# Stick-breaking layer: the output units of token half 0 woven into the last head pair's attention steps, their squares on GpSimd

## The reference

```python
h = rmsnorm(x, norm_g[2])
q, k, v, g = jnp.split(h @ w_in, 4, axis=-1)        # 16 heads of 64
for i in range(S // BLOCK_Q):
    z = jnp.einsum('bqhd,bkhd->bhqk', q[:, q0:k_end], k[:, :k_end]) * scale
    log_beta = jax.nn.log_sigmoid(z)
    log_1m_beta = jnp.where(strict, jax.nn.log_sigmoid(-z), 0.0)
    after = lax.cumsum(log_1m_beta, axis=3, reverse=True) - log_1m_beta
    a = jnp.where(strict, jnp.exp(log_beta + after), 0.0)
    o = jnp.einsum('bhqk,bkhd->bqhd', a, v[:, :k_end])
x = x + (o * jax.nn.silu(g)) @ w_out
h = rmsnorm(x, norm_g[3])                           # the next layer's norm
```

## Time and profile before

| | us |
|---|---|
| median of 3 runs | 2641.67 |
| lowest, highest | 2639.49, 2642.42 |
| the profiled execution | 2638.96 |
| its span in the trace | 2637.1 |
| PE busy in the span | 2371.8 |
| VectorE busy | 1571.1 |
| ScalarE busy | 1350.4 |
| GpSimd busy | 463.5 |

### The profile page before, as it was taken

The page is one execution under the profiler, slowest core; times in us unless marked ns, Lnnn a source line. Parts: engine busy times, 40 slices in busy tenths (PEclk is TensorE's granted clock), DMA queues, the critical chain, the costliest instruction groups (busy, mean ns, idle before and its releaser), DMA issues. The chain is left out here.

```text
span 2637.1 us, 43259 instructions
## 1 busy us (share of the span) xinstructions
PE 2371.8 (90%) x17364; PEld 1342.9 (51%) x17364; DVE 1571.1 (60%) x2220; ACT 1350.4 (51%) x2029; POOL 463.5 (18%) x418
## 2 busy tenths in 40 slices
PE   8999988988788888889888899999998899999887
PEld 4666644444444444544444455555544346766443
DVE  5565565676556656656546566666666365657655
ACT  4433433445554454454433777777878444344342
POOL 0000111132012012011011233323223210101011
PEclk9999999998899999999989999999999899999989
DMA  3011112213333434433431211112120111111113
GB/s 114 31 35 41 33 33 72 80 54 71 88 71 82 85 68 86 82 73 90 82 83 56 63 50 43 47 49 57 49 57 25 64 59 41 41 33 34 40 48 120
DMA packets 197722, 160.31 MB, mean 61 GB/s; under 512 B 160115, under 2 KB 161395, under 8 KB 197525
## 3 DMA queue, kind: packets, MB, share of 16 engines
q1 hardware_dynamic: 193428, 153.35, 22.1%
q0 software_dynamic: 4096, 4.20, 0.6%
HBM read 98.79 MB, written 4.19 MB: 39 GB/s over the span
## 5 line engine op out<-in xcount | busy, mean ns | idle before, releaser
L240 PE MATMUL psum<-h_hi,w_hi 128*128 128x512 f16 x1128 | 432.7, 384 | 35.9 <-ACT mla_silu_g L285 18.6
L241 PE MATMUL psum<-h_lo,w_hi 128*128 128x512 f16 x1128 | 431.8, 383 | 0.0
L242 PE MATMUL psum<-h_hi,w_lo 128*128 128x512 f16 x1128 | 431.4, 382 | 0.0
L2343 DVE SCALAR_TENSOR_TENSOR w_lo<-wf,w_hi 128x1024 f16<-128x1024 f32 (+3 forms) x194 | 231.4, 1201 | 137.5 <-ACT w_hi L2338 137.3
L256 PE MATMUL psum<-w_hi,h_hi 128*128 128x128 f16 x1504 | 256.9, 220 | 0.0
L257 PE MATMUL psum<-w_lo,h_hi 128*128 128x128 f16 x1504 | 256.6, 219 | 0.0
L258 PE MATMUL psum<-w_hi,h_lo 128*128 128x128 f16 x1504 | 256.6, 219 | 0.0
L1619 ACT ACTIVATE ssum<-psum,mla_neg_top 128x128 f32<-128x128 f32 (+7 forms) x128 | 94.7, 740 | 297.1 <-DVE mla_neg_top L1526 297.1
L1097 POOL TENSOR_TENSOR sb_al<-sb_zc,sb_ah 128x256 f16<-128x256 f32 (+2 forms) x96 | 166.2, 1731 | 373.1 <-ACT sb_ah L1062 373.1
L2338 ACT ACTIVATE w_hi<-wf 128x1024 f16<-128x1024 f32 (+3 forms) x194 | 187.1, 975 | 37.5 <-PE psum L242 18.3
L240 PEld LDWEIGHTS psum<-h_hi,w_hi 128*128 128x128 f16 x1128 | 111.3, 99 | 157.1 <-issue 39.7
(11 more groups left out here) (320 smaller groups left out, 5874.4 us busy)
## 6 DMA issues: line engine op xcount, KB each, us to landing
wf<-in_gla_out SPq DMA_DIRECT2D x32, 512.0 KB, 3.5
wf<-in_sb_in SPq DMA_DIRECT2D x32, 512.0 KB, 3.5
wf<-in_mla_out SPq DMA_DIRECT2D x20, 512.0 KB, 3.8
wf<-in_gla_v SPq DMA_DIRECT2D x16, 512.0 KB, 3.5
wf<-in_gla_g SPq DMA_DIRECT2D x16, 512.0 KB, 3.5
wf<-in_mla_gate SPq DMA_DIRECT2D x16, 512.0 KB, 3.7
wf<-in_sb_out SPq DMA_DIRECT2D x16, 512.0 KB, 3.5
xT<-in_x_T SPq DMA_DIRECT2D x16, 256.0 KB, 4.7
```

Source lines behind the costliest of these rows:

```text
L240: pe.matmul(out, wh[:, w], act_hi[:, k, tok], start=(i == 0), stop=False)
L241: pe.matmul(out, wh[:, w], act_lo[:, k, tok], start=False, stop=False)
L242: mm = pe.matmul(out, wl[:, w], act_hi[:, k, tok], start=False, stop=(i == last))
L2343: dve.scalar_tensor_tensor(out=self.w_lo[s % Layer.NSPLIT][:, 0:cols], in0=self.wf[s % Layer.NLOAD][:, 0:cols], scalar=W_SCALE, in1=self.w ...
```

## The change

In the last pair the list is built in three pieces. Steps 84 and 85 are as before, and so is step 86 but for its filler, which is gone. From step 87 (`OUT_FROM` = 3) to step 89 the opening parts of three output units of half 0, (0, 0) to (2, 0), are the filler (`OPENED` = 3). From step 90 (`HALF_DONE` = 6) on, the closing u items of these three and the five other units of half 0 are the filler. Behind the step of pv 94 come the three opening parts of unit (0, 1), then pv 95, then the three opening parts of unit (1, 1), then all that remains of half 1. The slab items move with their units. A unit of half 0 now waits only for the y blocks of half 0 (`2 * last block + c + 1`; the y blocks are finished in the order pair, half).

In `Residual` with `pool_half=0` the squares of half 0 are made by GpSimd, as a product of xT with itself, between the al items; ScalarE makes them for half 1 only. The scratch tiles are in `sg[:, 0, :]` (the gate buffer of even pairs), since zc[0] is in use as long as the attention runs. ScalarE's wait for al_ready before the first square is gone. Two semaphores of the MLA layer are moved to `Net`, which changes no instruction's order.

```diff
--- before.py
+++ after.py
@@ -549,10 +549,12 @@
 class Residual:
 
 
-    def __init__(self, layer, sq):
+    def __init__(self, layer, sq, pool_half=None):
+
         L = self.layer = layer
-        self.sq = sq
+        self.sq, self.pool_half = sq, pool_half
         self.sq_ready, self.sum_ready = L.sem("sq_ready"), L.sem("sum_ready")
+        self.pool_sq_ready = L.sem("pool_sq_ready")
 
     def dve(self, dve, n):
         L = self.layer
@@ -565,7 +567,7 @@
     def act(self, act, n):
         L = self.layer
         _, (k, c, final, *_), _, b = L.units[n]
-        if not final:
+        if not final or c == self.pool_half:
             return
         act.wait_ge(L.acc_free[b], L.turn[n])
         if k == 0:
@@ -585,11 +587,20 @@
         eng.wait_ge(self.sum_ready, (c + 1) * (KD - 1))
 
     def pool(self, pool, n):
-        _, (k, c, final, *_), _, _ = self.layer.units[n]
-        if not final or k == 0:
+        L = self.layer
+        _, (k, c, final, *_), _, b = L.units[n]
+        if not final:
             return
-        s = self.layer.net.ssum[:, c * HALF:(c + 1) * HALF]
-        pool.wait_ge(self.sq_ready, c * KD + k + 1)
+        s = L.net.ssum[:, c * HALF:(c + 1) * HALF]
+        if c == self.pool_half:
+            x = L.net.xT[:, k, c * HALF:(c + 1) * HALF]
+            L.wait_unit(pool, n)
+            pool.tensor_tensor(s if k == 0 else self.sq[k % 2], x, x, ALU.mult).then_inc(self.pool_sq_ready, 1)
+            pool.wait_ge(self.pool_sq_ready, k + 1)
+        if k == 0:
+            return
+        if c != self.pool_half:
+            pool.wait_ge(self.sq_ready, (c if self.pool_half is None else 0) * KD + k + 1)
         if k > 1:
             pool.wait_ge(self.sum_ready, self.sums_before(k, c))
         pool.tensor_tensor(s, s, self.sq[k % 2][:], ALU.add).then_inc(self.sum_ready, 1)
@@ -677,6 +688,8 @@
 
     PAIRS = SB_HEADS // 2
     SHIFT = 2
+    OUT_FROM, HALF_DONE = 3, 6
+    OPENED = 3
     CEILING = 40.0
     MASK = -60000.0
     MASK_GAIN = 32768.0
@@ -713,7 +726,7 @@
             self.consts = sem("consts")
             self.gate = Gate(L, "dve")
             self.split = Split(L)
-            self.resid = Residual(L, [self.zc[0][:, 0, :], self.zc[0][:, 1, :]])
+            self.resid = Residual(L, [self.sg[:, 0, 0:HALF], self.sg[:, 0, HALF:T]], pool_half=0)
             halves = [[t[:, c, :] for c in range(2)] for t in (self.zc[1], self.zc[2], self.zc[3], self.Lf[0])]
             self.handover = Handover(L, net, after, halves[0], halves[1], halves[2] + halves[3],
                                      self.resid.wait_sums, self.wait_out_slab)
@@ -783,6 +796,9 @@
                 out.append(("stack", name, p))
         return out + later
 
+    def out_banks(self, k, c):
+        return [5, 6, 7]
+
     def attention(self, p):
 
 
@@ -809,21 +825,33 @@
         filler = L.cut(self.projections(0, w_in, "g"), ("g",))
 
         main = []
+        final = self.PAIRS - 1
         for p in range(self.PAIRS):
             for i, step in enumerate(self.attention(p)):
                 if i == self.SHIFT:
                     items += weave(main, filler, lambda it: it[0] in ("u", "part"))
-                    filler = L.cut(self.projections(p + 1, w_in), ("q", "k", "v", "g")) if p + 1 < self.PAIRS else []
+                    filler = L.cut(self.projections(p + 1, w_in), ("q", "k", "v", "g")) if p < final else []
+                    main = []
+                if p == final and i == self.OUT_FROM:
+                    out = []
+                    for k in range(KD):
+                        out += L.slab(w_out[k], 1024, [("x", (k, 0, True))], self.out_banks(k, 0))
+                    filler, out = L.open_early(L.cut(out, ("x",)), self.OPENED)
+                    items += main
+                if p == final and i == self.HALF_DONE:
+                    items += weave(main, filler, lambda it: it[0] == "part")
+                    filler, main = out, []
+                if p == final and i == self.OUT_FROM:
                     main = []
                 main += step
 
         last = []
-        for c in range(2):
-            for k in range(KD):
-                last += L.slab(w_out[k], 1024, [("x", (k, c, True))], [5, 6, 7])
-        early, last = L.open_early(L.cut(last, ("x",)), 2)
-        items += weave(main, early, lambda it: it[0] == "part")
-        items += [("pv", self.PAIRS * len(self.STEPS) - 1)] + last
+        for k in range(KD):
+            last += L.slab(w_out[k], 1024, [("x", (k, 1, True))], self.out_banks(k, 1))
+        first, last = L.open_early(L.cut(last, ("x",)), 1)
+        second, last = L.open_early(last, 1)
+        items += weave(main, filler, lambda it: it[0] in ("u", "part"))
+        items += first + [("pv", self.PAIRS * len(self.STEPS) - 1)] + second + last
         L.finish_items(self.handover.placed(self.place_products(items), L.units))
 
     def place_products(self, items):
@@ -863,7 +891,7 @@
             L.pe_begin_unit(pe, n, part)
             if name == "x":
                 k, c, _ = payload
-                pe.wait_ge(self.yl_ready, 2 * (L.share(n, part, KD)[-1] + 1))
+                pe.wait_ge(self.yl_ready, 2 * L.share(n, part, KD)[-1] + c + 1)
                 L.pe_feature_major(pe, n, part, self.y_hi, self.y_lo, range(KD), c)
                 return
             p, c = payload
@@ -1011,8 +1039,6 @@
             n, = a
             name, payload, _, b = L.units[n]
             if name == "x":
-                if n == L.last_unit_of[4 * self.PAIRS - 1]:
-                    act.wait_ge(self.al_ready, self.PAIRS * len(self.STEPS))
                 self.resid.act(act, n)
                 return
             p, c = payload
@@ -1088,7 +1114,10 @@
             pool.affine_select(out=self.mask_k[:], in_=self.mask_k[:], compare_op=ALU.is_ge, fill=0.0, base=0,
                                pattern=[[-1, P]], channel_multiplier=1).then_inc(self.consts, 1)
         elif kind == "u":
-            if L.units[a[0]][0] == "x":
+            name, payload, _, _ = L.units[a[0]]
+            if name == "x":
+                if payload[:2] == (1, 0):
+                    pool.wait_ge(self.yt_ready, 2 * (self.PAIRS - 1))
                 self.resid.pool(pool, a[0])
         elif kind == "a":
             s, = a
@@ -1194,7 +1223,7 @@
             self.csq_ready, self.ctot, self.cr_ready = sem("csq_ready"), sem("ctot"), sem("cr_ready")
             self.chi, self.clo = sem("chi"), sem("clo")
             self.ra_ready, self.rsum, self.rhi, self.rlo = sem("ra_ready"), sem("rsum"), sem("rhi"), sem("rlo")
-            self.stacked = [sem("stacked_even"), sem("stacked_odd")]
+            self.stacked = net.queries_staged
             self.s_ready, self.top_ready, self.neg_ready = sem("s_ready"), sem("top_ready"), sem("neg_ready")
             self.p_ready, self.inv_ready = sem("p_ready"), sem("inv_ready")
             self.ph_ready, self.pl_ready = sem("ph_ready"), sem("pl_ready")
@@ -2321,6 +2350,7 @@
         self.w_loaded = [ctx.enter_context(nc.semaphore(f"w_loaded{i}")) for i in range(Layer.NLOAD)]
         self.w_hi_done = ctx.enter_context(nc.semaphore("w_hi_done"))
         self.w_lo_done = ctx.enter_context(nc.semaphore("w_lo_done"))
+        self.queries_staged = [ctx.enter_context(nc.semaphore(f"queries_staged{i}")) for i in range(2)]
         self.guests_from = 0
         self.psum = ctx.enter_context(nc.psum_tensor("psum", [P, 8, HALF], F32))
```

## The result

| | before | after |
|---|---|---|
| median, us | 2640.58 (2637.5 to 2642.42, 4 runs) | 2621.39 (2619.72 to 2622.91, 4 runs) |
| ratio | | 0.9928, 95% interval 0.9911 to 0.9946 |
| profiled execution, its span | 2638.96, 2637.1 | 2622.91, 2621.2 |
| stretch: t of step 86 to unit (2, 1) | 110.02 | 89.46 |
| waits of PE in the stretch | 20.8 | 7.3 |

A forecast was written before the change was run, and what follows sets the result against it. PE was taken as starved of filler in the last pair by latency chains and a lower clock. 76.9 + 5.2 + 4.0 + 1.5 + 2.0 + 2.8 = 92.4 us against 110.0, 17.6 less: median 2624 us, range 2616 to 2634.

The forecast's parts named there:

- PE work, 76.9 us: Matmuls from step 86's t to unit (2, 1): output units 51.8, attention 24.2, norm 0.9 us, unchanged by the edit.
- The start, 4.0 us: In step 86, its filler gone, PE stands about 4.0 us ahead of the t of step 87.
- Switches 5.2: Small gaps where PE changes between kinds of item: 0.52 us a step over ten steps, 5.2 us.
- slow clock 1.5: From the t of step 87, its four matmuls and the first filler run at the lower clock, costing about 1.5 us.
- Order inside a step 2.0: VectorE's queue zc, xT, w_lo, subtraction just keeps up with c; step 90's doubled additions and w_lo cost 2.0 us.
- exclusion 2.8: GpSimd's squares and sums hold up VectorE's two-input w_lo by 0.7 us a step, 2.8 us over four steps.
- That is level, with nothing to spare: In a full step the subtraction ends at 8.0 us and PE reaches c, which needs it, at 7.9.
- The square at 1.30 us: GpSimd's square, not in the trace, was taken to last as long as the sum of the same shape, 1.30 us.
- The end: PE's waits for al ahead of pv 94 and pv 95 and for y_lo ahead of unit (0, 0) vanish.
- Edits at nothing: ScalarE's eight lost squares of 0.63 us, moved loads, banks and the shorter y-block wait were priced at no time.
- Behind 2114: After the first matmul of unit (2, 1), both programs were taken as alike except for the tile of ScalarE's squares.
- rival 3: Gain given back later: half 1 or the next layer waits, less than 5 us of gain remains; chance 0.05.

The follow-up runs named there:

- e_fill86: The changed kernel with the filler begun one step earlier, from step 86 (OUT_FROM 2 in place of 3): 2619.86 us, ratio 0.9926.
- k_both: The changed kernel with filler from step 86 on and the w_hi and w_lo of steps 90 to 95 moved later: 2618.04 us, ratio 0.9901.
- c_pool_only: The kernel before, its item order kept, with only the squares of half 0 on GpSimd and the shorter y-block wait: 2639.85 us, ratio 0.9996.
- b_act_squares: The changed kernel, its woven order kept, with the squares of half 0 given back to ScalarE: 2627.43 us, ratio 0.9947.
- i_newton_behind: The changed kernel with the norm's three Newton steps on VectorE behind the addition of unit (1, 1), not ahead of it: 2620.32 us, ratio 0.9908.
- j_both_newton: The changed kernel with filler from step 86, w_hi and w_lo moved later, and Newton steps behind unit (1, 1)'s addition: 2617.13 us, ratio 0.9893.
- d_short_squares: The changed kernel with GpSimd's squares (except the first) and sums of half 0 on 8 of 512 columns: 2620.97 us, ratio 0.9922.
- g_ns_early: The changed kernel with the norm of half 0 put one item earlier, ahead of the closing of unit (0, 1): 2625.73 us, ratio 0.9941.

## Why the prediction was right, and which terms were off

The median came to 2621.39 us, where 2624 was predicted and 2616 to 2634 given. The mechanism was right: the last pair was starved of filler, and the output units of half 0 fill it. That the total came so near is in part luck. The stretch took 2.9 us less than predicted, but 4.6 us came back ahead of it and behind it, which the prediction had at nothing, so the profiled execution took 2622.91 us where the sum gave 2621.4. The prediction then put the median 2.7 us above the profiled execution, and it came 1.5 us below it. By the prediction's own steps, with 92.4 us predicted for the stretch and 89.5 measured:

- *PE work, 76.9 us.* No instruction of PE was added or lost (17364 on both pages).
- *The start, 4.0 us.* 1.31 + 2.69 = 4.0, as said, though 1.31 of it stand ahead of the c of step 86, and `e_fill86` shows that most of it was only a lack of filler.
- *Switches 5.2 and slow clock 1.5.* What remains of the stretch after work and waits is 89.46 - 76.9 - 7.32 = 5.2. Two kernels ran the stretch at a clock of 1.00 throughout. In `k_both` the same remainder is 83.05 - 76.9 - 2.7 = 3.45, in `e_fill86`, whose full steps are in the order of the change, it is 86.16 - 76.9 - 5.20 = 4.06. So the switches, mis-sized at 5.2, are 3.5 to 4.1, and the slow clock is an estimate of 1.2 to 1.8 us. The row of the changed kernel from the t of step 87 on agrees: 8% of 19.45 us are 1.6.

```profile
2011.55:2031.00 19.45, 19.45 (x108) 9.21 (x110) 11.96 (x15) 12.17 (x20) 7.58 (x5) 0.92 0.18 55
2031.00:2098.00 67.00, 63.55 (x312) 27.01 (x313) 39.19 (x37) 38.74 (x40) 34.31 (x22) 1.00 0.20 65
```

- *Order inside a step 2.0, exclusion 2.8.* Together 4.8, measured 3.3, but the shares were wrong. The step that failed is "w_lo should lose part of one operation ... Four steps: 2.8 us": taking GpSimd's work away gives 0.6 us. w_lo and Ll do lose, Ll 1.07 us in step 91, but mostly where VectorE has time left. The sign that was named, w_lo at over 1.5 us just ahead of a wait of c, didn't show: it took 1.23 to 1.45 us in steps 91 to 94. "That is level, with nothing to spare" was right for steps 92 and 93 (0.30 and 0; step 95 has no c). The order costs 1.76 in step 91, behind the doubled additions and w_lo for which the prediction took its 2.0, and most of the 1.26 in step 94, where two w_lo stand in a row, which the prediction hadn't seen. Without the squares' work these two are 1.76 and 1.05, so the order is 2.8 us, where 2.0 were predicted, and the exclusion 0.5, where 2.8 were.
- *The square at 1.30 us.* It takes 1.04 alone and 1.9 to 2.1 behind a two-input operation of VectorE, 1.47 on the mean.
- *The end.* "Nothing is left of the three waits": so it is.
- *Edits at nothing.* "ScalarE loses eight squares ..., which hid beside matmuls anyway" was wrong for the order to which the change moves. In the order of before they cost nothing (`c_pool_only`), in the woven order 4 us (`b_act_squares`). The sum was not hurt, since it was built with the squares on GpSimd; the sentence on what this part of the change is worth was.
- *Behind 2114.* The prediction took the programs to run alike there; instead 1.8 us came back as a wait for w_lo. Before, the units of half 1 closed one at a time, 5.2 us apart, and VectorE still waited for PE ahead of the additions of units (1, 1) and (2, 1), 0.33 and 0.79 us. With the change units (0, 1) and (1, 1) close 2.2 us apart, with the norm between them, and the loop over ScalarE and VectorE starts late. `i_newton_behind` shows this for 1.1 of the 1.8 us; for the rest it is argued. This is rival 3 at a small size, and "a new wait behind 2114" was one of the signs of being wrong.

The Trainium skill, "SBUF — State Buffer", section "Who interferes with whom", states that a VectorE instruction with two SBUF inputs excludes a GpSimd one that reads SBUF, and that the one issued first holds the other up. By that, the traces agree in both directions: Ll 2.29 us for 1.22 with GpSimd first, the square 2.09 for 1.04 with VectorE first, and the clamp, whose input is in PSUM, keeps its 1.21. The rule says nothing of whether it costs time; here that was 0.6 us of 89.5.

The layers ahead of and behind the stretch moved by 1.0 and 1.8 us with the same instructions; the last section says what is known of it. Where the medians of `c_pool_only`, `k_both` and `j_both_newton` lost what their stretches gained stays open.

## What to carry to other kernels

Where PE is starved by a chain of latencies and independent work stands right behind it, count the stall and fill it with that work; then read each in-order queue for what stands ahead of the operation that PE waits for, since an operation in front of it that itself waits can cost more than a lock between two engines (here w_lo, moved for 3.2 us in the stretch, where the lock cost 0.6). An operation that costs nothing in one order may cost in another: price it in the new order, by what waits behind it on its engine. And follow the units behind the filled place as far as the next slack, because work that now closes in a burst can turn a loop that had time to spare into the bound.

## What the runs showed of the hardware

A GpSimd product of a tile with itself, 128x512 f32, takes 1.04 us alone, where the sum of two different tiles of that shape takes 1.27.

The same 781 matmuls of a GLA head take 85.48 us at a clock of 1.00 or 86.88 at 0.98, in one execution; which heads get the lower clock differs from run to run. It is a source of steps of about 1.4 us in the span. In the 14 traces here, layer 3 from its first full unit to the end of the span took 467.7 us (`d_short_squares`, 33 us of it at the lower clock level) to 472.8 us (`g_ns_early`, 47 us), with the same 3472 matmuls, and its time follows the time at the lower level closely (correlation 0.97). The layers ahead of the stretch took 2001.8 to 2007.7 us and follow it more loosely (0.81). So small effects here are read from the stretch and not from the median. Two heads of layer 3 in the changed kernel:

```profile
2201.29:2288.17 86.88, 81.74 (x781) 55.58 (x780) 53.71 (x70) 35.45 (x53) 7.78 (x4) 0.98 0.12 37
2374.82:2460.30 85.48, 80.19 (x781) 55.16 (x780) 53.63 (x70) 35.39 (x52) 7.53 (x5) 1.00 0.12 38
```
